# Attention value products with exchanged operands in a two-block transformer kernel

## What is computed

```python
s = jnp.einsum('bqhd,bkhd->bhqk', q, k) * scale      # scores
p = jax.nn.softmax(jnp.where(mask, s, NEG_INF), axis=-1)
o = jnp.einsum('bhqk,bkhd->bqhd', p, v)               # the value products
```

## Time and profile before

| | |
|---|---|
| median of 3 runs | 1343.16 us (1342.54 to 1346.32) |
| the profiled execution | 1343.7 us |
| its span | 1341.7 us |
| mean granted TensorE clock | 0.944 |
| TensorE matmuls | busy 1210.3 us, 90% of the span, 5840 records |
| TensorE weight loads | busy 674.1 us, 5840 records |
| VectorE / ScalarE / GpSimd busy | 534.3 / 450.9 / 96.5 us |
| value products (L956) | busy 128.1 us, 880 records |
| probability transposes (L993) | busy 85.0 us, 440 records |

### The profile page before, as it was taken

One profiled execution on the slowest core, in us unless ns is written; L12 is line 12 of the kernel. 1 busy time (PEld: TensorE's weight loads), 2 busy tenths in 40 slices (PEclk: granted clock), 3 DMA queues, 4 the chain that ended last, 5 costly groups with the idle time before them and its releaser, 6 DMA issues.

```text
span 1341.7 us, 16334 instructions
## 1 busy us (share of the span) xinstructions
PE 1210.3 (90%) x5840; PEld 674.1 (50%) x5840; DVE 534.3 (40%) x1385; ACT 450.9 (34%) x1175; POOL 96.5 (7%) x107
## 2 busy tenths in 40 slices
PE   4899989999879898979999998998999799978895
PEld 1565634555554443334455555564544365635562
DVE  2334323344553211334452334112224742575665
ACT  0122324354441102222244331213333453455543
POOL 0000000000010000000000000000000000275523
PEclk9999989999889999989999998998999899978897
DMA  9421345470004402432111002332111101100001
GB/s 348 145 67 32 134 150 188 157 235 17 1 0 109 64 17 63 84 102 63 63 64 63 1 0 94 86 112 93 48 47 48 47 34 55 39 1 0 34 3 63
DMA packets 60407, 99.66 MB, mean 74 GB/s; under 512 B 12084, under 2 KB 22145, under 8 KB 60328
## 3 DMA queue, kind: packets, MB, share of 16 engines
q1 hardware_dynamic: 54514, 93.58, 22.6%
q10 hardware_dynamic: 5814, 5.04, 1.2%
HBM read 96.47 MB, written 4.08 MB: 75 GB/s over the span
## 4 chain that ended last, share of the span: by engine, by line
PE 78%; DVE 12%; ACT 5%; issue 2%; DMA 1%; ACTq 1%; DVEq 0%; SPq 0%
PE PR L926 33%; PE OB L956 6%; PE SC L978 6%; PE PT L819 5%; PE PR L819 5%; PE OB L819 5%; PE SC L819 4%; PE PT L993 3%; PE PR L881 3%; DMA ring<-in_w_ada 1%; PE PR L1016 1%; DVE stage L1837 1%; DVE tok L1837 1%; DVE d L2146 1%; PE PR L834 1%
## 5 line engine op out<-in xcount | busy, mean ns | idle before, releaser
L926 PE MATMUL PR<-ring,hT 128*128 128x512 f32 (+1 forms) x784 | 377.9, 595 | 6.0 <-ACT hT L1289 3.5
L1466 ACT ACTIVATE stage<-stage,nmax 128x256 f32<-128x256 f32 (+7 forms) x200 | 103.7, 519 | 272.8 <-DVE nmax L2199 240.4
L926 PEld LDWEIGHTS PR<-ring,hT 128*128 128x128 f32 x784 | 136.9, 198 | 107.2 <-issue 89.6
L956 PEld LDWEIGHTS OB<-arena,pts 128*128 128x128 f32 (+3 forms) x880 | 130.1, 198 | 99.1 <-issue 77.8
L926 PE MATMUL PR<-hT,ring 128*128 128x512 f32 (+1 forms) x304 | 150.1, 619 | 0.0
L956 PE MATMUL OB<-arena,pts 128*128 128x64 f32 (+4 forms) x880 | 128.1, 274 | 11.0 <-ACT pts L1289 11.0
L978 PE MATMUL SC<-arena 64*128 64x256 f32 (+15 forms) x432 | 111.5, 450 | 4.0 <-DVE nmax L2199 3.6
L1289 ACT ACTIVATE pts<-PT 128x256 f32<-128x256 f32 (+7 forms) x200 | 80.7, 404 | 101.2 <-PE PT L993 79.0
L993 PEld LDWEIGHTS PT<-ident,stage 128*128 128x128 f32 (+3 forms) x440 | 58.6, 144 | 102.6 <-issue 70.0
L993 PE MATMUL PT<-ident,stage 128*128 128x128 f32 (+3 forms) x440 | 85.0, 284 | 19.5 <-DVE stage L1845 11.0
L1734 POOL TENSOR_TENSOR arena<-arena 128x192 f32<-128x192 f32 (+1 forms) x45 | 37.0, 823 | 775.0 <-PE OB L956 759.5
(11 more groups left out here) (391 smaller groups left out, 1348.1 us busy)
## 6 DMA issues: line engine op xcount, KB each, us to landing
ring<-in_w_ada SPq DMA_DIRECT2D x12, 2048.0 KB, 8.5
ring<-in_od_w_in SPq DMA_DIRECT2D x8, 2048.0 KB, 16.6
ring<-in_w_in SPq DMA_DIRECT2D x5, 1536.0 KB, 6.9
ring<-in_ev_w_in SPq DMA_DIRECT2D x3, 2048.0 KB, 9.9
ring<-in_w_in SPq DMA_DIRECT2D x3, 2048.0 KB, 10.0
ring<-in_ev_w_out SPq DMA_DIRECT2D x2, 2048.0 KB, 10.1
ring<-in_od_w_out SPq DMA_DIRECT2D x2, 2048.0 KB, 7.7
ring<-in_w_out SPq DMA_DIRECT2D x2, 2048.0 KB, 7.9
```

Of the source, the lines that this page charges most:

```text
L926: mm = pe.matmul(dst, l, r, start=(k == 0), stop=(k == KT - 1))
L956: mm = pe.matmul(ob[:, h * w:h * w + w], pts[0:rows_, v % 2, n * P:n * P + P], vb, start=(n == 0), stop=(n == len(blocks) - 1))
L1466: give(act.activation(pb[:, s % NP, 0:n], zm[:, s % 2, 0:n], ACT.Exp, bias=nmax[:, row, c:c + 1], scale=-1.0, accum_out=rsum[:, row, c:c + ...
```

## The change

The two operands of each value product change places: the values are loaded as weights and the transposed probabilities are streamed, so the output is feature-major (`OT`, one bank) instead of token-major. With a value width of 64 only half of the array's columns are needed for one head, so two units are done together, one writing to the output partitions 0 to 63 and the other to 64 to 127. `values(v)` is now called for a pair of units and at every second step, between the first half of the filler and the transposes (before: for each unit, at the end of the step). For `dif` (width 128) the pair's products follow each other on the whole array. When a group is done, ScalarE copies `OT` to SBUF (`feature_major`, into `ots[L]`), TensorE transposes it back in blocks of 128 x 128 (`token_major_again`) into `OF`, the other bank, and VectorE's `finish_group` waits for that (`ob_done`) and reads `OF`. So the two banks no longer alternate between groups. `pv_done` counts pairs instead of units.

```diff
@@ -497,6 +497,8 @@
         zm = stage[:, 0:1024].rearrange("p (b n) -> p b n", b=2)
         pb = stage[:, 1024:3072].rearrange("p (b n) -> p b n", b=NP)
         z3 = a2["hgt"][:, 0:S]
+        OT, OF = OB
+        ots = [d3, arena[:, 17408:17920], grow[:, 512:1024]]
         frow = arena[0:NH, 16384:16896]
         nfrow = arena[0:NH, 16896:17408]
 
@@ -554,6 +556,8 @@
         pt_done = sem("pt_done")
         pt_ev = [sem(f"pt_ev{i}") for i in range(2)]
         pv_done = sem("pv_done")
+        ot_ev = sem("ot_ev")
+        ob_done = sem("ob_done")
         ob_free = sem("ob_free")
         y_s = sem("y_s")
         ye_s = sem("ye_s")
@@ -942,22 +946,42 @@
 
             def attention(L):
                 def values(v):
-                    L_, g, j, sus = v_units[v]
-                    su = sus[-1]
-                    ob = OB[g_no[L, g] % 2]
-                    if j == 0 and g_no[L, g] >= 2:
-                        pe.wait_ge(ob_free, g_no[L, g] - 1)
-                    pe.wait_ge(pt_ev[v % 2], v // 2 + 1)
-                    blocks = value_blocks(su)
-                    w = 128 if su[0] == "dif" else 64
-                    h = su[1] // 2 if su[0] == "dif" else su[1]
-                    for n, vb in enumerate(blocks):
-                        rows_ = blocks_seen(su[2]) if su[0] == "cmp" else P
-                        mm = pe.matmul(ob[:, h * w:h * w + w], pts[0:rows_, v % 2, n * P:n * P + P], vb,
-                                       start=(n == 0), stop=(n == len(blocks) - 1))
+                    L_, g, j, _ = v_units[v]
+                    if j == 1 and g_no[L, g]:
+                        pe.wait_ge(ot_ev, g_no[L, g])
+                    pe.wait_ge(pt_ev[0], (v + 1) // 2)
+                    pe.wait_ge(pt_ev[1], (v + 1) // 2)
+                    pair = [v_units[u][3][-1] for u in (v - 1, v)]
+                    keys = [value_blocks(su) for su in pair]
+                    blocks = range(len(keys[0]))
+                    if pair[0][0] == "dif":
+                        order = [(r, n) for r in range(2) for n in blocks]
+                    else:
+                        order = [(r, n) for n in blocks for r in range(2)]
+                    for r, n in order:
+                        rows_ = blocks_seen(pair[r][2]) if pair[r][0] == "cmp" else P
+                        if pair[r][0] == "dif":
+                            dst = OT[:, (j - 1 + r) * P:(j + r) * P]
+                        else:
+                            dst = OT[MN * r:MN * r + MN, j // 2 * P:j // 2 * P + P]
+                        mm = pe.matmul(dst, keys[r][n], pts[0:rows_, (v - 1 + r) % 2, n * P:n * P + P],
+                                       start=(n == 0), stop=(n == len(keys[0]) - 1))
                     mm.then_inc(pv_done, 1)
 
-                first = True
+                def token_major_again(g):
+                    no, kind, units = g_no[L, g], plan[L][g][0], len(plan[L][g][2])
+                    pe.wait_ge(ot_ev, no + 1)
+                    if no:
+                        pe.wait_ge(ob_free, no)
+                    pairs = units if kind == "dif" else units // 2
+                    for p in range(pairs):
+                        dst = OF[:, p * P:p * P + P]
+                        if kind in SIDE_BY_SIDE:
+                            dst = OF[:, 0:units * MN].rearrange("p (r j d) -> p j r d", r=2, d=MN)[:, p]
+                        tr = pe.transpose(dst, ots[L][:, p * P:p * P + P], ident[:, :])
+                    tr.then_inc(ob_done, 1)
+
+                whole = None
                 counts, _ = schedule[L]
                 fill = (None for _, tiles in FILLERS[L] for t in tiles for _ in tile_matmuls(t))
 
@@ -976,8 +1000,15 @@
                             pe.wait_ge(masked, s - 1)
                         q, k, _, _, n = score_operands(s_units[s][2])
                         pe.matmul(SC[s % 2][:, 0:n], q, k, start=True, stop=True).then_inc(s_done, 1)
+                    if whole is not None:
+                        token_major_again(whole)
+                        whole = None
                     more = counts[r] if r < len(counts) else 0
                     filler(more // 2)
+                    if j % 2 == 0 and r:
+                        values(v - 1)
+                        if j == 0:
+                            whole = g - 1
                     su = sus[-1]
                     s = s_no[su]
                     if su[0] in ("dif", "cmp"):
@@ -994,10 +1025,8 @@
                                           ident[:, :])
                     tr.then_inc(pt_done, 1)
                     filler(more - more // 2)
-                    if not first:
-                        values(v - 1)
-                    first = False
                 values(v)
+                token_major_again(len(plan[L]) - 1)
 
             def mixed_late(i):
 
@@ -1436,9 +1465,20 @@
                 def transposed(v, sus):
                     act.wait_ge(pt_done, v + 1)
                     if v >= 2:
-                        act.wait_ge(pv_done, v - 1)
+                        act.wait_ge(pv_done, v // 2)
                     r, w = transposed_shape(sus[-1])
                     give(copy(pts[0:r, v % 2, 0:w], PT[v % 2][0:r, 0:w]), pt_ev[v % 2], v // 2 + 1)
+                    _, g, j, _ = v_units[v]
+                    if j == 0 and g:
+                        feature_major(g - 1)
+
+                def feature_major(g):
+                    no, (kind, _, units) = g_no[L, g], plan[L][g]
+                    n = P * (len(units) if kind == "dif" else len(units) // 2)
+                    act.wait_ge(pv_done, (last_v[L, g] + 1) // 2)
+                    if no:
+                        act.wait_ge(ob_done, no)
+                    give(copy(ots[L][:, 0:n], OT[:, 0:n]), ot_ev, no + 1)
 
                 for r_, (v, (_, g, j, sus), new) in enumerate(steps(L)):
                     if sus[-1][0] == "sb":
@@ -1481,6 +1521,7 @@
                                 next(chains[-1])
                     if L == 2 and r_ in HG_EARLY:
                         exponentials(HG_EARLY.index(r_))
+                feature_major(len(plan[L]) - 1)
                 close_behind(v)
 
             def exponentials(c):
@@ -1724,7 +1765,7 @@
             pool.memset(ones[:, :], 1.0).then_inc(pool_seq, 1)
             pool.wait_ge(pool_seq, 1)
             pool.memset(tbl[32:33, :], NEG).then_inc(pool_seq, 1)
-            pool.wait_ge(pv_done, last_v[0, len(plan[0]) - 1] + 1)
+            pool.wait_ge(pv_done, (last_v[0, len(plan[0]) - 1] + 1) // 2)
             drained(pool, ("adag", 1, 1))
             pool.memset(a1["fqT"][MN:MN + 2, :, :], 1.0).then_inc(pool_seq, 1)
             pool.memset(a1["fkT"][MN:MN + 2, :, :], 1.0).then_inc(pool_seq, 1)
@@ -1791,7 +1832,7 @@
 
             nsa = [g for g, e in enumerate(plan[2]) if e[0] != "sb"][-1]
             pool.wait_ge(hgf, 3)
-            pool.wait_ge(pv_done, last_v[2, nsa] + 1)
+            pool.wait_ge(pv_done, (last_v[2, nsa] + 1) // 2)
             pool.wait_ge(masked, s_no["sb", 0, 0])
             differences(0)
             drained(pool, ("hq", 2))
@@ -2083,8 +2124,8 @@
             def finish_group(L, g, part=0):
                 kind, i, vus = plan[L][g]
                 no = g_no[L, g]
-                dve.wait_ge(pv_done, last_v[L, g] + 1)
-                ob, row = OB[no % 2], no % 16
+                dve.wait_ge(ob_done, no + 1)
+                ob, row = OF, no % 16
                 if kind in ("mla", "swa", "fox"):
                     den = rsum[:, row, :]
                     if kind == "swa":
```

## The result

| | before | after |
|---|---|---|
| median of 4 runs | 1342.85 us (1339.79 to 1346.32) | 1355.47 us (1352.31 to 1358.54) |
| profiled execution, its span | 1343.7, 1341.7 us | 1355.7, 1354.2 us |
| mean granted TensorE clock | 0.944 | 0.942 |

The changed kernel takes 1.0087 times as long as the one before, with a 95% interval of 1.0064 to 1.0111. The forecast was 1350 us in a range of 1336 to 1366, slower more likely than not. Direction and range hold, the mechanism holds in kind, and the likeliest value is 5.5 us too low. Two of its terms were each off by more than that, in opposite directions, as shown further down.

A forecast was written before the change was run, and what follows sets the result against it. TensorE was taken as the bound, busy 90% of the span with 78% of the chain. Products -17.9, turning transposes +11.9, waits +12 and layer end +1 gave +7.0 on 1343.7: forecast 1350 us, range 1336 to 1366.

The forecast's parts named there:

- Products: Value products of 92 width-64 pairs on TensorE: halves overlap, 0.30 us for each burst, -17.9 us in all.
- full factor of two: Rival on value products: bursts cost nothing beyond their columns, 1310 us; chance 0.03.
- separate halves: Rival on value products: the two column halves don't overlap, +43 us, near 1393 us; chance 0.06.
- Turning transposes: 108 new transposes on TensorE between scores and filler, at 0.11 us each, +11.9 us.
- Waits: TensorE waits for ScalarE's copies before turning transposes (+11) and value products (+5), taken as +12 us, bounds 4 to 25.
- the two discounts: In the waits: some 5 us already standing at two long waits left out, then 12 of the remaining 16 us taken.
- New place: Value products lose cover at their earlier place, so ScalarE's copy is late at three places: +5 us.
- Ends of layers: Last copy and transposes: hidden under VectorE in layer 1, 1 us (0 to 3) at the end of layer 2.
- Waits spread to the clock: Rival: VectorE and ScalarE get late in turn, TensorE's layer 2 waits lose clock, 1366 us; chance 0.17.

The follow-up runs named there:

- e_place: Kernel before, with old value products called at the new place, two units together, no copy or turning back: 1348.7 us, ratio 1.0018 to before.
- e_noturn: Changed kernel without output copy and turning back, VectorE reading the feature-major output from two alternating banks: 1331.59 us, ratio 0.9895 to before.
- e_nowait: Changed kernel with turning transposes reading the identity matrix, so not waiting for ScalarE's copy, which stays: 1338.49 us, ratio 0.9946 to before.
- e_nodif: Changed kernel with the four `dif` groups in their old form and place: 1355.83 us, ratio 1.0085 to before.
- e_long: Changed kernel with only `mla` and `fox` groups of three or four key blocks exchanged, ScalarE's output copy first: 1343.25 us, ratio 0.9989 to before.
- e_after: The changed kernel timed again, unaltered, beside the other runs: 1356.66 us, ratio 1.0080 to before.
- e_copyfirst: Changed kernel with ScalarE copying the finished output before the next group's first probabilities: 1351.23 us, ratio 1.0037 to before.
- e_turnlate: e_copyfirst with turning transposes moved behind the step's probability transposes, except after `swa` and `dif` groups: 1350.39 us, ratio 1.0038 to before.
- e_long_cmp: e_long with the four `cmp` groups of layer 2 exchanged too: 1344.39 us, ratio 1.0007 to before.
- e_order: Changed kernel with all key blocks of a pair's first unit before those of the second: 1370.45 us in a single execution.

## Why the prediction came out as it did

- *Products: right.* The forecast was -17.9 us; the runs give -16.5 for the exchange. Each price per pair is within 0.02 of the timeline, with 0.09 us on the way from the whole array to the halves and 0.05 on the way back. In the earlier trace rows the quarter strips gave the right price for halves. The *full factor of two* and *separate halves* are out. That the totals agree is partly luck. By the account the traces give 24.7 us: there the old products took 105.1 us for 91.8 at the prices of the earlier trace rows, because many groups stand in a stretch of lower clock or before a score on 64 rows (0.93 instead of 0.84 for four blocks). From e_place to e_noturn it is 26.2 us, and 6.7 us of waits, which I had not priced for this step, brought it back towards the forecast. How much of the extra saving is the clock of single executions isn't known.
- *Turning transposes: 0.11 us assumed, 0.135 measured.* 14.6 us instead of 11.9. I priced them as members of a stream of transposes. Behind a wait or a score on 64 rows four take 0.49 instead of 0.44, and three groups at a granted clock of 0.50 take 1.3 us more than priced. Without the waits (e_nowait) all 108 take 12.8 us.
- *Waits: right in kind, too small in size.* This is the term that was furthest off: +12 forecast, +23 of idle time in the trace. What I had worked out place by place came: eleven short waits before turning transposes at the inner group ends, 6.3 us, and two long ones of 5.9 and 3.7; the trace has ten of 0.2 to 1.3 us, 6.6 together, and two of 5.92 and 2.78. Three at the ends of layers add 2.0. The mistake is in the two discounts, 5 us for waits that stand there already and 4 of the 16 in the next step, which assumed that a place can't lose twice. In layer 2 three waits of 4.8 to 5.9 us follow each other where there were three of 2.4 to 3.6. The value products and probability transposes together wait only 2.1 us more (25.2 + 7.4 after, 11.0 + 19.5 before), and the rest 3.5.
- *New place: +5 forecast, +2.4 measured*, by e_place.
- *Ends of layers: right for layer 1, at its upper bound for layer 2.* At the end of layer 1 I called copy and transposes hidden under VectorE:

```profile
811.55 1.09 PE L967 MATMUL OB<-pts,arena 128*64 128x128 f32 x16
...
812.74 0.60 ACT L1318 ACTIVATE arena<-OB 128x512 f32<-128x512 f32 x1 [2.16 <-PE OB L967]
...
813.39 0.65 PE L981 MATMUL OB<-ident,arena 128*128 128x128 f32 x4 [0.75 <-ACT arena L1318]
...
814.30 0.20 DVE L2134 RECIPROCAL fr<-rsum 128x8 f32<-128x8 f32 x1
...
816.21 0.63 PE L838 MATMUL OB<-ident,tok 128*128 128x128 f32 x4 [2.16 <-DVE tok L1878]
```

  And before, behind the products at 804.65 of the earlier trace rows:

```profile
809.41 1.08 PE L834 MATMUL OB<-ident,tok 128*128 128x128 f32 x4 [2.86 <-DVE tok L1837]
```

  TensorE waits 0.75 us for the copy, and 2.16 instead of 2.86 us for VectorE. From the start of the last products to its next work it is 4.66 us, where it was 4.76: hidden. After the last probability transpose of layer 2 the kernel takes 105.8 us where it took 102.7: +3, the upper bound that I gave for the +1. That time alone scatters between kernels (99.0 in e_nodif, 106.3 in e_long, which has no copy there), but one wait before small matmuls of the recurrence shows the cost:

```profile
1264.12 0.54 PE L1224 MATMUL PT<-arena 64*32 64x32 f32 x35 [4.34 <-issue]
```

  It was 1.72 us before, is 1.4 to 1.8 in e_place, e_noturn and e_long, without a copy at that end, and 3.9 to 4.5 us in every kernel with all groups, or all but `dif`, exchanged and copied.
- *Waits spread to the clock: no.* Between 1040 and 1110 us the granted clock is 0.88 (0.90 before). The slots of matmuls that fall in its stretches at the lower level add up to 11.8 us there (12.0 before, 12.2 in e_after): the low stretches are longer (17.1 us, 13.7 before), but the longer waits fill the difference.

So by the three runs: +2.4 - 16.5 + 24.8 = +10.7 us, against +5 - 17.9 + 19.9 = +7.0 in the forecast (with turning back and its waits, 11.9 + 7 + 1, as the last term). By the runs, the copy, its wait and the turning transposes together are the mis-sized step, 4.9 us too cheap; by the traces the waits are 11 us and the products' saving 7 us larger than forecast, and the two errors offset each other in part.

What stays open: how the 25 us of turning back divide. e_nowait says 18 for the waits and 7 for the rest, the records say 14.6 for the transposes and net idle time of 7 to 10. Both can't be exact. e_nowait and e_copyfirst show that the wait for the copy costs time. How the 4.9 us that were missing in the forecast divide between this wait and the dearer transposes (2.7 by the trace) is not shown.

## What to carry to other kernels

Exchanging the operands to fill both column halves paid (16.5 us here), but the output then has the other layout, and turning it back costs a copy on another engine between two pieces of TensorE's work: that round trip cost more than the products gave. Price such a round trip by the queue of the engine that copies, put the copy first in it, and don't discount new waits against old ones in a stretch where that engine is already behind, unless a trace shows that the old ones go. Before restricting a change to where records say that it gains, look at who sets the pace there: shortening a wait (e_turnlate) or saving work in front of one (e_long_cmp) gained nothing here.

## What the runs showed of the hardware

- Records on two column halves overlap only when they alternate: a four-block pair takes 1.03 us alternating and 1.51 us one half after the other. In the single execution of e_order this is 12.6 us in the products' slots and some 14 us of time.
- Going from the whole array to column halves costs the matmul before it 0.09 us (0.95 instead of 0.86), and going back costs the four transposes behind it 0.05 (0.49 instead of 0.44).
- After a wait of 5.69 us twelve records take 1.48 us (1083.09 to 1084.57) instead of 0.81. The granted clock of this stretch is 0.50, the lower level. Before the change six records took 1.44 us at 0.50 behind the wait of 3.61 us.
